# A two-layer transformer trunk on one core: the activations' transposes made 128 partitions wide, their blocks moved between partition quarters by DMA

## The reference

```python
D_MODEL, SEQ, D_FF = 2048, 256, 5632

def swiglu(x, wg, wu, wd):
    return (jax.nn.silu(x @ wg) * (x @ wu)) @ wd

# layer 0: h += pooling mixer (4 groups of 512 x 512 weights)
# layer 1: h += attention(rmsnorm(h) @ w_q, shared k and v) @ w_o
h = h + swiglu(rmsnorm(h, ffn_norm[layer]), w_gate[layer], w_up[layer], w_down[layer])
# after both layers: rmsnorm(h, final_norm)
```

## Time and profile before

| | us |
|---|---|
| median of 3 runs (1734.56 to 1735.6) | 1734.8 |
| the profiled execution | 1734.48 |
| its span, first to last instruction | 1732.7 |
| PE busy | 1720.7 (99%) |
| PEld busy | 1418.1 (82%) |
| DVE busy | 1068.7 (62%) |
| ACT busy | 805.6 (46%) |
| POOL busy | 57.1 (3%) |
| DMA: 326.36 MB, mean 188 GB/s | |

### The profile page before, as it was taken

The page is one execution under the profiler, slowest core; times in us unless marked ns, Lnnn a source line. Parts: engine busy times, 40 slices in busy tenths (PEclk is TensorE's granted clock), DMA queues, the critical chain, the costliest instruction groups (busy, mean ns, idle before and its releaser), DMA issues.

```text
span 1732.7 us, 21002 instructions
## 1 busy us (share of the span) xinstructions
PE 1720.7 (99%) x7828; PEld 1418.1 (82%) x7828; DVE 1068.7 (62%) x1343; ACT 805.6 (46%) x1062; POOL 57.1 (3%) x65
## 2 busy tenths in 40 slices
PE   9999999999999999999999999999999999999998
PEld 8888888888888888888777888888888888888887
DVE  7666666666666444555676656666666666654554
ACT  6544444444444443446665554444444444444443
POOL 1100000000000000002010100000000000000000
PEclk9999999999999999999999999999999999999999
DMA  8565665555555655555434555565665655665562
GB/s 291 185 194 193 192 193 191 192 192 192 191 193 175 204 194 170 205 201 177 145 122 147 194 176 194 192 193 193 193 193 193 193 194 194 206 207 185 178 212 104
DMA packets 163145, 326.36 MB, mean 188 GB/s; under 512 B 5652, under 2 KB 5780, under 8 KB 162840
## 3 DMA queue, kind: packets, MB, share of 16 engines
q1 hardware_dynamic: 162944, 324.67, 56.7%
q10 hardware_dynamic: 152, 1.06, 0.2%
HBM read 323.61 MB, written 2.10 MB: 188 GB/s over the span
## 4 chain that ended last, share of the span: by engine, by line
PE 96%; DVE 2%; ACT 1%; DMA 1%; SPq 0%; issue 0%; DVEq 0%
PE acc L998 32%; PE acc L1000 31%; PE acc L999 31%; PE acc L1018 1%; DMA raw<-pool_w_in 1%; DVE w_lo L637 0%; PE acc L1147 0%; PE acc L1175 0%; DVE prob L852 0%; PE acc L1162 0%; ACT prob L490 0%; ACT w_hi L340 0%; PE acc L1126 0%; DVE mx L833 0%; PE acc L1033 0%
## 5 line engine op out<-in xcount | busy, mean ns | idle before, releaser
L632 DVE TENSOR_TENSOR w_lo<-raw,w_hi 128x1024 fp32r<-128x1024 f32 x584 | 703.3, 1208 | 563.6 <-ACT w_hi L337 560.2
L337 ACT ACTIVATE w_hi<-raw 128x1024 fp32r<-128x1024 f32 x584 | 604.9, 1037 | 787.8 <-PE acc L1000 785.3
L998 PE MATMUL acc<-w_hi,xT_hi 128*128 128x512 f32 x1568 | 613.0, 391 | 0.0
L1000 PE MATMUL acc<-w_hi,xT_lo 128*128 128x512 f32 x1568 | 610.3, 389 | 0.0
L999 PE MATMUL acc<-w_lo,xT_hi 128*128 128x512 f32 x1568 | 610.2, 389 | 0.0
L998 PEld LDWEIGHTS acc<-w_hi,xT_hi 128*128 128x128 f32 x1568 | 294.4, 188 | 63.0 <-issue 1.5
L1000 PEld LDWEIGHTS acc<-w_hi,xT_lo 128*128 128x128 f32 x1568 | 294.3, 188 | 61.4
L999 PEld LDWEIGHTS acc<-w_lo,xT_hi 128*128 128x128 f32 x1568 | 294.4, 188 | 60.1
L998 PE MATMUL acc<-w_hi,hT_hi 128*128 128x512 f32 x858 | 335.9, 391 | 1.4 <-DVE w_lo L632 1.4
L1000 PE MATMUL acc<-w_hi,hT_lo 128*128 128x512 f32 x858 | 334.0, 389 | 0.0
L999 PE MATMUL acc<-w_lo,hT_hi 128*128 128x512 f32 x858 | 333.9, 389 | 0.0
(11 more groups left out here) (115 smaller groups left out, 431.1 us busy)
## 6 DMA issues: line engine op xcount, KB each, us to landing
raw<-w_gate_in SPq DMA_DIRECT2D x88, 1024.0 KB, 5.2
raw<-w_up_in SPq DMA_DIRECT2D x88, 1024.0 KB, 5.2
raw<-w_down_in SPq DMA_DIRECT2D x64, 1024.0 KB, 5.0
raw<-w_down_in SPq DMA_DIRECT2D x32, 768.0 KB, 4.3
raw<-w_q_in SPq DMA_DIRECT2D x16, 1024.0 KB, 5.1
raw<-w_o_in SPq DMA_DIRECT2D x16, 1024.0 KB, 5.1
raw<-pool_w_in SPq DMA_DIRECT2D x4, 1024.0 KB, 12.3
raw<-w_kv_in SPq DMA_DIRECT2D x4, 1024.0 KB, 5.0
```

The lines of the kernel that those rows point to most:

```text
L337: nc.scalar.activation(w_hi[:, i % RING, 0:tiles * C], slot, ACT.Copy).then_inc(hi_ready, 1)
L632: nc.vector.tensor_tensor(w_lo[:, i % RING, 0:tiles * C], slot, w_hi[:, i % RING, 0:tiles * C].bitcast(F32), ALU.subtract).then_inc(unit_r ...
L998: nc.tensor.matmul(dst, at_hi[:, k, tok], w_hi[:, w, cols], start=first and kk == 0, stop=False)
L1000: last = nc.tensor.matmul(dst, at_lo[:, k, tok], w_hi[:, w, cols], start=False, stop=end)
```

## The change

Each block's activations are transposed by two DVE instructions over all 128 partitions, one for each token tile. Such an instruction transposes every 32 x 32 block within its own quarter of the partitions, so it leaves the blocks in the wrong quarter. They go to a new view `hT_x`, which lies in the memory of `hT_hi`. SP then issues 16 DMAs within SBUF (`act_exchange`), one for each pair of source quarter and destination quarter, that carry the blocks to `hT_f`: 32 partitions x 2 pieces of 512 bytes each, 32 KB. For this the layout of a block changes: before, the four feature tiles of a block lay one behind the other, 256 tokens each; now token and feature tile are interleaved, token s of tile k at 4 s + k (`quad_block`). The matmuls of down read their stationary operand with a step of four elements (`quad_tile`). Gate, up, query, pooling and o read theirs as before.

The semaphore `at_full` now counts the DMAs (256 for each block); `at_turned` tells SP that the transposes are done. SP issues the exchange after load 5 of the block, and its loop over j is peeled for that.

```diff
+        hT_x = at("hT_x", [P, KF, S], F32, o_hi)
...
+        def quad_block(x, j):
+            return x[:, bass.ds(4 * j, 4), :].rearrange("p k s -> p (k s)")
+
+        def quad_tile(x, k, t):
+            return quad_block(x, k // 4).rearrange("p (t s k) -> p t s k", t=T, k=4)[:, t, :, k % 4]
...
+            def act_exchange(l, j):
+
+                sp.wait_ge(at_turned, NFB * l + j + 1)
+                for pb in range(4):
+                    for q in range(4):
+                        src = quad_block(hT_x, j).rearrange("c (t q x) -> c t q x", t=T, q=4)
+                        dst = quad_block(hT_f, j).rearrange("c (t b x) -> c t b x", t=T, b=4)
+                        sp.dma_start(dst[q * QUAD:(q + 1) * QUAD, :, pb, :],
+                                     src[pb * QUAD:(pb + 1) * QUAD, :, q, :]).then_inc(at_full, 16)
...
                         load(LAP_GU[l] + 2 * j, 4 * m + i, w, k0, a + b, j * C)
+                        if 4 * m + i == 5 and not (isinstance(j, int) and j == 0):
+                            act_exchange(l, j - 1)
...
                     load(LAP_DOWN[l] + 3 * b, i, down_v[l], k0, a + c, b * C)
+                    if i == 5 and isinstance(b, int):
+                        act_exchange(l, NFB - 1)
...
-                ac.wait_ge(at_full, NFB * l + j + 1)
+                ac.wait_ge(at_full, 256 * (NFB * l + j) + 256)
...
-            def act_turn(l, j, pb):
+            def act_turn(l, j):
 
                 ve.wait_ge(job_out, JOB_GU[l] + 2 * j + 2)
-                src = act[pb * QUAD:(pb + 1) * QUAD, :, :].rearrange("r t (k q c) -> r t k q c", k=4, q=4)
-                for q in range(4):
-                    dst = hT_f[q * QUAD:(q + 1) * QUAD, 4 * j:4 * j + 4, :].rearrange("c k (t b r) -> c t k b r", t=T, b=4)
-                    last = nc.vector.transpose(dst[:, :, :, pb, :], src[:, :, :, q, :])
-                if pb == 3:
-                    last.then_inc(at_full, 1)
+                for t in range(T):
+                    src = act[:, t, :].rearrange("r (k q c) -> r k q c", k=4, q=4)
+                    dst = quad_block(hT_x, j).rearrange("c (t q r k) -> c t k q r", t=T, q=4, k=4)[:, t, :, :, :]
+                    last = nc.vector.transpose(dst, src)
+                last.then_inc(at_turned, 1)
...
-                    if not first and 3 <= i < 7:
-                        act_turn(l, j - 1, i - 3)
+                    if not first and i == 3:
+                        act_turn(l, j - 1)
...
+                        x_hi, x_lo = at_hi[:, k, tok], at_lo[:, k, tok]
+                        if quad:
+                            x_hi, x_lo = quad_tile(at_hi, k, t), quad_tile(at_lo, k, t)
...
-                        nc.tensor.matmul(dst, at_hi[:, k, tok], w_hi[:, w, cols], start=first and kk == 0, stop=False)
+                        nc.tensor.matmul(dst, x_hi, w_hi[:, w, cols], start=first and kk == 0, stop=False)
...
-                        nc.tensor.matmul(dst, hT_hi[:, k, tok], w_hi[:, w, cols], start=begin, stop=False)
+                        nc.tensor.matmul(dst, quad_tile(hT_hi, k, T - 1), w_hi[:, w, cols], start=begin, stop=False)
```

More of the change, by code:

```diff
@@ L210, in trunk @@
         t_free = [sem(f"t_free{b}") for b in range(2)]
+        at_turned = sem("at_turned")
         at_full = sem("at_full")
@@ L295, in _ @@
                     sp.dma_start(ropes[:, :, :, :], rope).then_inc(small_in, 16)
-            with sp.Fori(0, NFB) as j:
+            load_gate_up(0, 0)
+            with sp.Fori(1, NFB) as j:
                 load_gate_up(0, j)
-            with sp.Fori(0, NBLK) as b:
+            load_down(0, 0)
+            with sp.Fori(1, NBLK) as b:
                 load_down(0, b)
@@ L310, in _ @@
                     load(LAP_O + b, i, o_v, k0, a + c, b * C)
-            with sp.Fori(0, NFB) as j:
+            load_gate_up(1, 0)
+            with sp.Fori(1, NFB) as j:
                 load_gate_up(1, j)
-            with sp.Fori(0, NBLK) as b:
+            load_down(1, 0)
+            with sp.Fori(1, NBLK) as b:
                 load_down(1, b)
@@ L808, in down @@
                         up_out(l, NFB - 1)
-                    if first and 3 <= i < 7:
-                        act_turn(l, NFB - 1, i - 3)
+                    if first and i == 3:
+                        act_turn(l, NFB - 1)
                     if first and i == 9:
@@ L986, in _, with product @@
         def _(te):
-            def product(lap, i, at_hi, at_lo, k0, tiles, pair, first, last_unit, tokens=range(T), item=None):
+            def product(lap, i, at_hi, at_lo, k0, tiles, pair, first, last_unit, tokens=range(T), item=None, quad=False):
                 te.wait_ge(unit_ready, 8 * lap + i + 1)
@@ L995, in product @@
                         tok = slice(t * P, (t + 1) * P)
+                        x_hi, x_lo = at_hi[:, k, tok], at_lo[:, k, tok]
+                        if quad:
+                            x_hi, x_lo = quad_tile(at_hi, k, t), quad_tile(at_lo, k, t)
                         dst = pair_bank(pair, t)
                         end = last_unit and kk == tiles - 1
-                        nc.tensor.matmul(dst, at_hi[:, k, tok], w_hi[:, w, cols], start=first and kk == 0, stop=False)
-                        nc.tensor.matmul(dst, at_hi[:, k, tok], w_lo[:, w, cols], start=False, stop=False)
-                        last = nc.tensor.matmul(dst, at_lo[:, k, tok], w_hi[:, w, cols], start=False, stop=end)
+                        nc.tensor.matmul(dst, x_hi, w_hi[:, w, cols], start=first and kk == 0, stop=False)
+                        nc.tensor.matmul(dst, x_hi, w_lo[:, w, cols], start=False, stop=False)
+                        last = nc.tensor.matmul(dst, x_lo, w_hi[:, w, cols], start=False, stop=end)
                         if item is not None and kk == tiles - 1 and t == 0:
@@ L1099, in down @@
                         te.wait_ge(at_lo, NFB * (l + 1))
-                    product(LAP_DOWN[l] + 3 * b, u, hT_hi, hT_lo, k0, tiles, job % 2, u == 0, u == UF - 1)
+                    product(LAP_DOWN[l] + 3 * b, u, hT_hi, hT_lo, k0, tiles, job % 2, u == 0, u == UF - 1, quad=True)
                     if u == 2 and not first and l == 0:
@@ L1254, in _ @@
                 last = product(LAP_DOWN[1] + 3 * (NBLK - 1), u, hT_hi, hT_lo, k0, tiles,
-                               (JOB_DOWN[1] + NBLK - 1) % 2, u == 0, u == UF - 1, tokens)
+                               (JOB_DOWN[1] + NBLK - 1) % 2, u == 0, u == UF - 1, tokens, quad=True)
                 if u == UF - 1 and 0 in tokens:
                     last.then_inc(tile0_done, 1)
-            tok = slice((T - 1) * P, T * P)
             for part in range(2):
@@ L1268, in _ @@
                         end = u == UF - 1 and kk == tiles - 1
-                        nc.tensor.matmul(dst, hT_hi[:, k, tok], w_hi[:, w, cols], start=begin, stop=False)
-                        nc.tensor.matmul(dst, hT_hi[:, k, tok], w_lo[:, w, cols], start=False, stop=False)
-                        last = nc.tensor.matmul(dst, hT_lo[:, k, tok], w_hi[:, w, cols], start=False, stop=end)
+                        nc.tensor.matmul(dst, quad_tile(hT_hi, k, T - 1), w_hi[:, w, cols], start=begin, stop=False)
+                        nc.tensor.matmul(dst, quad_tile(hT_hi, k, T - 1), w_lo[:, w, cols], start=False, stop=False)
+                        last = nc.tensor.matmul(dst, quad_tile(hT_lo, k, T - 1), w_hi[:, w, cols], start=False, stop=end)
                     if part == 1:
```

## The result

The changed kernel takes 1755.99 us (median of 4 runs, 1755.65 to 1756.6) against 1734.9 for the kernel before: ratio 1.0122, 95% interval 1.011 to 1.0134, 21.1 us. The forecast was no change. The profiled execution's span is 1753.9 us, 21.2 more than before.

A forecast was written before the change was run, and what follows sets the result against it. TensorE's matmuls, their count times their beat, were taken to bound the kernel. Every term on the path was 0, so 1734.8 us, no change (1734 to 1736, chance 0.62); range 1732 to 1770.

The forecast's parts named there:

- What bounds the kernel: Whole kernel: TensorE, busy 99% of the span; time is the count of matmuls times their beat, 0.227 us in down.
- the relief of DVE: Gate and up blocks: 153.4 us of narrow transposes leave VectorE; no TensorE wait goes with them, worth 0.
- the term of the stationary operand read with a stride: Down's matmuls and tail: a strided weight load, even doubled to 213 ns, stays under the matmul; 0.
- below nothing there is no room: Down's matmuls: load and matmul already overlap and the beat is the matmul's own columns, so hidden loads cost 0.
- Rival C: Down stage: the load outgrows the matmul beyond a factor of two; +28 us (1763) to +232 (1967) or more; chance 0.17.
- C's small end: Down stage: the load outgrows the matmul only slightly, costing below +35 us; chance 0.05.
- Rival B: Weight loads' rate halves: nothing in 2094 matmuls, the 36 of the tail go 0.120 to 0.227 us; +3.3, 1738.1; chance 0.12.
- The exchange: Each block: 16 DMAs issued in 7.2 us, landed by 147.6 to 148.4, over 6 us to spare; 0.
- The point from which it shows, 154.8: Worked block: latest landing of the exchange before TensorE feels it at unit 9.
- The transposes: Each block: two wide VectorE transposes at 0.87 us each, 1.75 each if strided writes go at half rate.

The follow-up runs named there:

- second probe: Kernel before with extra unread matmuls at the end: 512 to 448 columns at steps 1, 2, 4; 256 to 64 at steps 1 to 16; no time given.
- first probe: Kernel before with 504 extra unread matmuls at the end of TensorE's program, 12 for each pair of 64 to 512 columns and step 1 to 16; no time given.

## Why the prediction was wrong

**What bounds the kernel**: right. The time moved by the beat of the matmuls and by nothing else; the relief of DVE (1068.7 to 953.5 us busy) was worth 0, as the run with adjacent reads shows at 1734.53.

**The step that failed** is the term of the stationary operand read with a stride, taken as 0, "the price both of no effect and of a factor of two". It measured 21.7 us: 17.9 in the 2094 matmuls of 512 columns, 3.8 in the tail. Two things in it were wrong.

The first is a size. I took a load's length as 107 ns, by removing the matmul's 13 ns from the tail's 120, and doubled it: 213, no more than the columns' 213, inside a beat of 226.7. The load is 112 ns long and the step makes it 233, a factor of 2.09. Two errors of some 4% each, on a case that stood on the edge, took it 6.7 ns past the beat. The bound from above had been used as if it were the length, with its overhead left off.

The second is the overlap itself: "below nothing there is no room", that is, a load that fits under its matmul costs nothing. At 512 columns this is false. There a beat of 233 to 235 ns comes also with steps of 2, 3 and 16, whose loads (118, 173 and 218 ns) are all shorter than the 227 ns of the plain beat. So most of the 8.3 ns would have come without the load outgrowing the matmul. At step 4 the load's length alone would give 233.3 as well, and 235.0 is measured, so how the two share the 8.3 ns can't be told by these runs; why the matmul is slowed stays open. In the tail, with 256 columns, it is the length alone: there step 2 takes 120 ns as step 1 does, and step 4 the 233 of its load.

**Rival C** had half of the mechanism, with 0.17: past the beat, each ns costs 2.1 us. The measured 1756 lies within the stated range of 1732 to 1770, but it was there for C's small end, which had 0.05. Its point, a factor of two, was right (226.7 / 112 = 2.03); what speaks against it, that the load has twice its time in reserve, is what fell. **Rival B** had the tail right: +3.3 forecast, +3.8 measured alone; its claim that the 2094 show nothing fell.

**The rule of the Trainium skill.** The prediction cites the Trainium skill, SBUF — State Buffer, Door 1: The DMA port swizzle, the note on cachelines. The first half of that note (two accesses to a 16 byte line for full bandwidth, each crossing pays) agrees with the loads: 118 ns at two to a line, 233 at one, beside 112 at four. The second half, four fp32 as a free stride, does not: that is the stride which cost 21.7 us. And at two to a line the load is nearly free, but the kernel isn't: 13.8 us.

**The exchange.** The issue was sized at 0.45 us from the three stores at the end of the kernel. It is 12.47 / 16 = 0.78, of which 0.63 is the instruction. at_full came at 152.1, not 148.4; the spare was 2.7 us, not 6, and ACT waited 3.8 us, not some tenths. Load 6 left at 150.88, not 145.2, and load 7 at 151.5, 3.1 us later than before, where I had it not moved. All of it stayed hidden, so this zero is right, but with less than half of the reserve that I gave it: at 0.95 us for each DMA it would have failed ((12.47 + 2.7) / 16). The point from which it shows, 154.8, stood the test of 32 DMAs, 7.2 us late against a wait of 7.1. That a small DMA lands 2.4 us after issue was on the safe side: 1.9.

**The transposes.** 1.09 us each, between my 0.87 and the upper bound of 1.75; off the path.

## What to carry to other kernels

Where every matmul has its own weight load, ask for a load's length by itself, not for the room that it has: the beat is never shorter than the longer of the two, and here they were 112 and 227 ns, so a factor of two was already too much. And don't take the room as free: with 512 columns a stepped load of 118 ns, half of the beat, already cost 7 ns a matmul. Keep the stationary operand's columns adjacent and let the interleaving fall on whoever has time to spare: the DMA took pieces of 128 bytes in place of 512 at no cost, and DVE even gained. Relief for an engine for which nobody waits is worth nothing; count the issues that it adds on the queue.

## What the runs showed of the hardware

- A weight load of 128 fp32r columns takes 112 ns at a step of 1, 118 at 2, 173 at 3, 233 at 4, 238 at 8, 218 at 16 (second probe, 64 columns, full clock): some 1.82 ns for each 16 byte piece that it touches, from step 2 to 4.
- A stepped load slows the matmul of 512 columns beside it, even where it is short itself: 226.7 ns become 233.3 at step 2, 235 at step 3 and 235 at step 16. At step 2 and 496 columns 2 ns of it are left, at 480 none; at step 4 480 columns take 240 ns. Why is open.
- At the 1.2 GHz level (granted clock 0.50, first probe, 128 columns) a load of step 1 took 213 ns, where it takes 112 at the full clock; one of step 4 took 233 at both.
- A DMA within SBUF over 32 partitions costs SP 0.63 us for the instruction and 0.78 with what lies between, with 64 pieces as with 256 (0.37 for a load of 1 MB). Half its size costs 0.55 and 0.70. Why it costs more than the load of 1 MB, no run here shows.
